# A diffusion-style block on one core: the second norm's factor at eviction, its shift as two extra columns of the up products

## The reference

```python
h  = rms(x, norm1_w) * (1 + scale1) + shift1
mixed = concat(s5(h @ w_in), attention(h @ w_in)) @ w_out
x  = x + gate1 * mixed
h2 = rms(x, norm2_w) * (1 + scale2) + shift2          # shift1 .. gate2 = silu(c) @ w_ada + b_ada
x  = x + gate2 * (silu(h2 @ w_ffn_gate) * (h2 @ w_ffn_up)) @ w_ffn_down     # "ffn1"
...                                                   # "ffn2", a pooling and attention mixer, "ffn3"

def _rms(x, w):
    y = x * lax.rsqrt(jnp.mean(x * x, axis=-1, keepdims=True) + 1e-6)
    return y * w
```

## Time and profile before

| | |
|---|---|
| median of 3 runs | 3241.77 us (3239.71 to 3243.99) |
| profiled execution | 3239.56 us |
| its span, mean granted clock of TensorE | 3237.8 us, 0.981 of full speed |
| read from memory | 627.53 MB, 194 GB/s over the span |

### The profile page before, as it was taken

How to read it: one execution, slowest core, us unless ns; L and a number is a source line. 1 busy time by engine, 2 the same in 40 slices (tenths; PEclk the granted TensorE clock), 3 DMA queues, 4 the chain that set the end, 5 groups by cost and what they waited for, 6 DMA issues and landing times.

```text
span 3237.8 us, 55997 instructions
## 1 busy us (share of the span) xinstructions
PE 3160.1 (98%) x24634; PEld 3021.9 (93%) x24634; DVE 1776.1 (55%) x1610; ACT 1236.9 (38%) x1162; POOL 153.3 (5%) x182
## 2 busy tenths in 40 slices
PE   6799999899999999999999999999999999999999
PEld 3599978899999999999999999999999998998997
DVE  0699865766444545654444544555556544454454
ACT  2376633433333333433333333343334333333333
POOL 1534100000000000000000000000030000000000
PEclk7799999999999999999999999999999999999999
DMA  9877667586555555555555555568635555555554
GB/s 343 295 252 239 240 228 239 194 279 226 184 184 191 183 184 192 174 178 171 180 170 179 170 177 174 174 181 148 129 128 183 181 189 180 190 181 189 188 181 156
DMA packets 329088, 631.88 MB, mean 195 GB/s; under 512 B 22452, under 2 KB 24264, under 8 KB 328664
## 3 DMA queue, kind: packets, MB, share of 16 engines
q1 hardware_dynamic: 317896, 626.16, 59.7%
q10 hardware_dynamic: 11040, 3.51, 0.5%
HBM read 627.53 MB, written 2.10 MB: 194 GB/s over the span
## 4 chain that ended last, share of the span: by engine, by line
PE 84%; DVE 2%; issue 1%; DMA 1%; ACT 1%; DVEq 0%; ACTq 0%
PE ps L576 21%; PE ps L577 21%; PE ps L578 21%; PE ps L606 3%; PE ps L608 3%; PE ps L607 3%; PE ps L2010 2%; PE ps L2012 2%; PE ps L2011 2%; PE ps L2047 1%; PE ps L2049 1%; PE ps L2048 1%; PE ps L1799 1%; PE ps L1800 1%; PE ps L1801 1%; DVE w_lo L443 1%
## 5 line engine op out<-in xcount | busy, mean ns | idle before, releaser
L443 DVE TENSOR_TENSOR w_lo<-raw,w_hi 128x2048 fp32r<-128x2048 f32 x496 | 1141.4, 2301 | 1246.5 <-ACT w_hi L438 1246.3
L438 ACT ACTIVATE w_hi<-raw 128x2048 fp32r<-128x2048 f32 x496 | 949.7, 1915 | 1700.9 <-PE ps L578 1308.7
L576 PE MATMUL ps<-act_hi,w_hi 128*128 128x256 f32 (+1 forms) x3328 | 949.8, 285 | 28.9 <-DVE act_lo L680 15.6
L577 PE MATMUL ps<-act_lo,w_hi 128*128 128x256 f32 (+1 forms) x3328 | 948.6, 285 | 0.0
L578 PE MATMUL ps<-act_hi,w_lo 128*128 128x256 f32 (+1 forms) x3328 | 946.8, 285 | 0.0
L576 PE MATMUL ps<-hid_hi,w_hi 128*128 128x256 f32 (+1 forms) x2816 | 795.8, 283 | 0.0
L577 PE MATMUL ps<-hid_lo,w_hi 128*128 128x256 f32 (+1 forms) x2816 | 795.4, 282 | 0.0
L578 PE MATMUL ps<-hid_hi,w_lo 128*128 128x256 f32 (+1 forms) x2816 | 794.3, 282 | 0.0
L576 PEld LDWEIGHTS ps<-act_hi,w_hi 128*128 128x128 f32 x3328 | 631.5, 190 | 31.1 <-issue 22.3
L577 PEld LDWEIGHTS ps<-act_lo,w_hi 128*128 128x128 f32 x3328 | 630.8, 190 | 0.0
L578 PEld LDWEIGHTS ps<-act_hi,w_lo 128*128 128x128 f32 x3328 | 630.6, 189 | 0.0
(11 more groups left out here) (370 smaller groups left out, 2754.2 us busy)
## 6 DMA issues: line engine op xcount, KB each, us to landing
...
```

Source lines behind the costliest of these rows:

```text
L438: act.activation(w_hi[b][:, :, :], raw[j % RING][:, :, :], ACT.Copy).then_inc(hi_ready, 1)
L443: dve.tensor_tensor(w_lo[b][:, :, :], raw[j % RING][:, :, :], w_hi[b][:, :, :].bitcast(F32), ALU.subtract).then_inc(lo_ready, 1)
L576: pe.matmul(o, whi, hi_, start=(k == 0 and not (shared and m % 2)), stop=False)
L577: pe.matmul(o, whi, lo_, start=False, stop=False)
```

## The change

The second norm is handled as the later ones: the products of `ffn1.up0`, `up1` and `up2` run on `res` times `gain` without `rstd`, and VectorE multiplies by `rstd` when either half is evicted. The shift has no place in that, so it is carried as a column of its own: the 16 columns ahead of the sequence are free in `act_hi` and `act_lo`, the last two of them (`SHIFT_COLS`) hold `shift2`, and all up products of `ffn1` have 258 moving columns (`UP1_COLS`). The result for the shift is column 1 of each bank. VectorE copies it to `up_bias` (`shift_out`); it is added as the bias of `Silu`, now four operations on `sig` in place of one from PSUM, and in the up half by four `scalar_tensor_tensor` in place of one product.

Quarters 0 and 1 of the norm's input are made behind the squares at `n` = 16 and 17 of `w_out` (`next_hi` on ScalarE, `next_lo` on VectorE), quarter 2 ahead of the split of the second chunk of `ffn1.up0` (`third_hi`), quarter 3 behind it. The four sums with `ones` stand ahead of the fourth chunk (`norm_pe`), mean and root at the fifth and sixth. Groups 2 and 3 of `w_out` are packed into banks 4 to 7 as 0 and 1 are in 0 to 3, and the last chunk is not run tile by tile any more. The gather of `scale2` moves from `n` = 18 to `n` = 14, into bank 0, and `gain` and the shift columns are made at `n` = 15 (`scale2_dve`). The diff, cut:

```diff
+SHIFT_COLS = slice(META - 2, META)
+UP1_COLS = slice(META - 2, T)
...
+        LATER = {"norm2": None, "ffn1_2": V_F1, "mix_2": V_MIX, "ffn2_2": V_F2}
+
+        def weight(name, k):
+            return gain[:, k:k + 1] if name == "norm2" else vecs[:, LATER[name] + k:LATER[name] + k + 1]
+
+        def normed_cols(name):
+            return SEQ_COLS if name == "norm2" else slice(0, T)
...
-                ins = act.activation(into(name)[0][:, k, :], res[:, k, :], ACT.Copy, scale=vecs[:, LATER[name] + k:LATER[name] + k + 1])
+                c = normed_cols(name)
+                ins = act.activation(into(name)[0][:, k, c], res[:, k, c], ACT.Copy, scale=weight(name, k))
...
-                q = hid0(p) + it
-                if deferred(p):
-                    act.wait_ge(bank_free[0], group_index(p, it, 0) + 1)
-                    n = cols.stop - cols.start
-                    act.activation(sig[:, :, 0:n], sig[:, :, 0:n], ACT.Silu).then_inc(sig_ready, 1)
-                    return
-                group_done(act, p, it, 0)
-
-                act.wait_ge(bank_free[1], group_index(p, it, 1))
-                act.activation(sig[:, :, 0:cols.stop - cols.start], bank(0, cols), ACT.Silu).then_inc(bank_free[0], 1)
-
-        def deferred(p):
-            return not p.name.startswith("ffn1")
+                n = cols.stop - cols.start
+                act.wait_ge(bank_free[0], group_index(p, it, 0) + 1)
+                if shifted(p):
+                    for m in range(4):
+                        ins = act.activation(sig[:, m, 0:n], sig[:, m, 0:n], ACT.Silu, bias=up_bias[:, 0, m:m + 1])
+                else:
+                    ins = act.activation(sig[:, :, 0:n], sig[:, :, 0:n], ACT.Silu)
+                ins.then_inc(sig_ready, 1)
+
+        def shifted(p):
+            return p.name.startswith("ffn1")
+
+        def up_bank(p, half, cols):
+
+            if shifted(p):
+                return ps[:, 4 * half:4 * half + 4, 2:2 + SEQ]
+            return bank(half, cols)
+
+        def shift_out(dve, p, half):
+            if shifted(p):
+                dve.tensor_copy(up_bias[:, half, :], ps[:, 4 * half:4 * half + 4, 1])
 
         def gate_dve(dve, p, it, g):
             cols = ffn_cols(p.name)
             n = cols.stop - cols.start
             q = hid0(p) + it
-            if g == 0 and deferred(p):
+            if g == 0:
 
                 group_done(dve, p, it, 0)
-                dve.wait_ge(hid_ready, q)
-                dve.tensor_tensor(sig[:, :, 0:n], bank(0, cols), per_token(cols), ALU.mult).then_inc(bank_free[0], 1)
+                if not (isinstance(q, int) and q == 0):
+                    dve.wait_ge(hid_ready, q)
+                shift_out(dve, p, 0)
+                dve.tensor_tensor(sig[:, :, 0:n], up_bank(p, 0, cols), per_token(cols), ALU.mult).then_inc(bank_free[0], 1)
             if g == 1:
                 group_done(dve, p, it, 1)
                 if not (isinstance(q, int) and q == 0):
                     dve.wait_ge(hid_ready, q)
-                if deferred(p):
-                    dve.tensor_tensor(val[:, :, 0:n], bank(1, cols), per_token(cols), ALU.mult).then_inc(bank_free[1], 1)
-                    dve.wait_ge(bank_free[1], group_index(p, it, 1) + 1)
-                    dve.wait_ge(sig_ready, q - sum(PARTS) + 1)
-                    dve.tensor_tensor(val[:, :, 0:n], sig[:, :, 0:n], val[:, :, 0:n], ALU.mult).then_inc(gate_mul, 1)
-                    dve.wait_ge(gate_mul, q - sum(PARTS) + 1)
+                shift_out(dve, p, 1)
+                dve.tensor_tensor(val[:, :, 0:n], up_bank(p, 1, cols), per_token(cols), ALU.mult).then_inc(bank_free[1], 1)
+                dve.wait_ge(bank_free[1], group_index(p, it, 1) + 1)
+                dve.wait_ge(sig_ready, q + 1)
+                if shifted(p):
+                    for m in range(4):
+                        ins = dve.scalar_tensor_tensor(out=val[:, m, 0:n], in0=val[:, m, 0:n], scalar=up_bias[:, 1, m:m + 1],
+                                                       in1=sig[:, m, 0:n], op0=ALU.add, op1=ALU.mult)
                 else:
-                    dve.wait_ge(bank_free[0], group_index(p, it, 0) + 1)
-                    dve.tensor_tensor(val[:, :, 0:n], sig[:, :, 0:n], bank(1, cols), ALU.mult).then_inc(bank_free[1], 1)
-                    dve.wait_ge(bank_free[1], group_index(p, it, 1) + 1)
+                    ins = dve.tensor_tensor(val[:, :, 0:n], sig[:, :, 0:n], val[:, :, 0:n], ALU.mult)
+                ins.then_inc(gate_mul, 1)
+                dve.wait_ge(gate_mul, q + 1)
...
                 cols = ffn_cols(f)
-                products(pe, f"{f}.up{i}", *((hid_hi, hid_lo) if f == "ffn3" else (act_hi, act_lo)), cols, counted(act_ready, ready0), norm if i == 0 else None)
+                if f == "ffn1" and i == 0:
+                    pe.wait_ge(gain_ready, 1)
+                    pe.wait_ge(shift_in, 2)
+                products(pe, f"{f}.up{i}", *((hid_hi, hid_lo) if f == "ffn3" else (act_hi, act_lo)), UP1_COLS if f == "ffn1" else cols,
+                         counted(act_ready, ready0), norm if i == 0 else None)
                 if f == "ffn3":
...
                 pending = run_phase(act, f"{f}.up{i}", split_hi, bind(act, gate_act), pending,
-                                    ahead={5: lambda: root_act(act, norm)} if norm and i == 0 else None)
+                                    ahead=({5: lambda: root_act(act, norm)} | ({1: lambda: third_hi(act)} if f == "ffn1" else {})) if i == 0 else None)
...
         def mean_root(dve, norm):
-            return {4: lambda: mean_dve(dve, norm, 4), 5: lambda: root_dve(dve, norm)}
+            return {4: lambda: mean_dve(dve, norm, 4), 5: lambda: root_dve(dve, norm)} | ({1: lambda: next_lo(dve, "norm2", 2)} if norm == "norm2" else {})
...
-            if g < 2:
-                return ps[:, 2 * g + m // 2, SEQ * (m % 2):SEQ * (m % 2) + SEQ]
-            return ps[:, (4, 0)[g - 2] + m, 0:SEQ]
+            return ps[:, 2 * g + m // 2, SEQ * (m % 2):SEQ * (m % 2) + SEQ]
 
         def first_free(g):
 
-            return bank_free[(0, 1, 1, 0)[g]], 1 + byname["w_out"].g0 // 2 + (1, 1, 2, 2)[g]
+            return bank_free[g // 2], 2 + byname["w_out"].g0 // 2 + g % 2
...
                 if n in (13, 14, 17):
-                    g = {13: 0, 14: 1, 17: 2}[n]
-                    act.wait_ge(*first_free(g))
-                    act.wait_ge(*((ssq_ready, QUADS + g) if g else (glu_mul, 2)))
-                    squares_act(act, g, 4 + g, T)
+                    first_squares(act, {13: 0, 14: 1, 17: 2}[n])
+                if n in (16, 17):
+                    act.wait_ge(gain_ready, 1)
+                    next_hi(act, "norm2", n - 16)
+
+        def first_squares(act, g):
+            act.wait_ge(*first_free(g))
+            act.wait_ge(*((ssq_ready, QUADS + g) if g else (glu_mul, 2)))
+            squares_act(act, g, 4 + g, T)
+
+        def third_hi(act):
+
+            act.wait_ge(chunk_done, byname["w_out"].before["S"] + 15)
+            next_hi(act, "norm2", 2)
 
...
+                    if n == 15:
+                        scale2_dve(dve)
+                    if n in (16, 17):
+                        next_lo(dve, "norm2", n - 16)
...
-            if m == 14:
-                pe.wait_ge(*first_free(2))
+            if m == 10:
+                pe.wait_ge(*first_free(0))
                 for g in range(4):
-                    gather(pe, accb2[:, g, :], 5, 4 * g)
-
-        def last_add(dve):
...
+        def scale2_dve(dve):
+
+            dve.wait_ge(mod_sum, 20)
+            link(dve, "dve", dve.tensor_tensor(gain[:, :], ps[:, 0, 0:16], bada[:, SCALE2:SCALE2 + 16], ALU.add))
+            link(dve, "dve", dve.tensor_scalar(gain[:, :], gain[:, :], 1.0, None, ALU.add))
+            dve.tensor_tensor(gain[:, :], gain[:, :], vecs[:, V_N2:V_N2 + 16], ALU.mult).then_inc(gain_ready, 1)
+            shift = mod[:, SHIFT2:SHIFT2 + KT].rearrange("p (k o) -> p k o", o=1).broadcast_to([P, KT, 2])
+            dve.tensor_copy(act_hi[:, :, SHIFT_COLS], shift).then_inc(shift_in, 1)
+            dve.wait_ge(shift_in, 1)
+            dve.tensor_tensor(act_lo[:, :, SHIFT_COLS], shift, act_hi[:, :, SHIFT_COLS].bitcast(F32), ALU.subtract).then_inc(shift_in, 1)
+            dve.wait_ge(gain_ready, 1)
...
-                pend = ffn_act(act, "ffn1", then(lambda: last_squares(act), lambda: norm_act(act, "norm2", 48)), squares_next_act(8, "ffn1_2"))
+                pend = ffn_act(act, "ffn1", then(lambda: first_squares(act, 3), lambda: next_hi(act, "norm2", 3)), squares_next_act(8, "ffn1_2"), "norm2")
...
-                pend = ffn_dve(dve, "ffn1", then(scale2, lambda: last_add(dve), lambda second: norm_dve(dve, "norm2", gain, 0, 48, second)), add_dve(("mod", 80)),
-                               squares_next_dve(8, "ffn1_2", add_dve(("mod", 80))))
```

(18 more changed lines are left out.)

56 lines of the change are left out of this document (13 added, 43 removed).

## The result

| | median us | range | runs |
|---|---|---|---|
| before | 3239.44 | 3237.18 to 3243.99 | 10 |
| changed | 3248.98 | 3242.93 to 3253.12 | 10 |

The ratio is 1.0030, 95% interval 1.0022 to 1.0039: slower by 9.5 us. 3248.0 was forecast, inside a range of 3237 to 3260. The profiled executions took 3239.56 and 3250.50 us, 10.9 apart, where the sum had given +6.2.

The account below looks back on a forecast made before the run. TensorE, busy 98% of the span, was taken to bound the kernel. 16.6 us removed against 19.6 added, plus 3.2 for the clock, made +6.2 on a median of 3241.77: 3248.0 us, range 3237 to 3260.

Parts of the forecast that it names:

- norm off the path, half clock, second pause: From the end of `w_out` into `ffn1.up0`: pauses and half-clock stretches around the second norm go, 16.6 us removed.
- two columns: All 4224 up products of `ffn1`: 258 columns instead of 256, on a straight line to 272, add 4.1 us.
- wait at `n` = 18: Last chunk but one of `w_out`: four `next_hi` ahead of its `w_hi` make TensorE wait 1.7 us.
- three boundaries with an ada chunk: Iteration boundaries of `ffn1.up0`: longer up-half eviction with an ada chunk grows the pause from 1.5 to 3.3, 5.5 us in all.
- seven S2 waits: Third chunk at seven later boundaries of `up1`, `up2` and their down parts: longer up-half eviction adds 4.0 us.
- eleven S6 waits: Seventh chunk of an iteration, behind the gate's eviction: four Silus instead of one delay it, eleven times, 4.0 us.
- first pass: Start of `ffn1.up0`: an addition, a sum of squares and an ada step ahead of the third chunk's `w_lo`, 0.3 us.
- clock behind three pauses: Behind the three longer pauses of `ffn1.up0`: half clock after two of three, 3.2 us, bounds 0 and 4.8.
- gather at its new place: In `w_out` at `n` = 14: costs the same 3.5 us and half-clock stretch as at its old place.
- column as the unit: Up products of `ffn1`: a product steps by single columns, 0.49 ns each, so two cost 0.98 ns per product.
- columns charged in steps: Rival for `ffn1`'s up products: 258 columns handled as 272, 29 us on top, time 3277; chance 0.13.
- all three: Rival: all three longer pauses of `ffn1.up0` lose the clock, 4.8 us instead of 3.2, time 3249.6; chance 0.12.

Follow-up runs that it names:

- Experiment 1: Changed kernel with other numbers and starts of moving columns (256 to 272) in the three up parts of `ffn1`; three single runs: 3251.2, 3257.6 and 3247.04 us.
- experiments 2: Changed kernel with one `Silu` without the gate's shift in `up1` and one product without the up half's shift in `up2`; 3244.64 us, single run.
- 3: Ada chunks of `up0` moved so that none stands behind an eviction: on the changed kernel 3237.31 us, on the kernel before 3234.75 us.
- 5: Changed kernel with VectorE's up-phase evictions in two pieces, the product by `rstd` ahead of the second chunk's split; 3233.04 us, 0.9975 of before.
- 4: Changed kernel with quarter 1 of the norm's input made one chunk later, at `n` = 18 behind that chunk's split; 3245.1 us, single run.
- experiment 7: Changed kernel with later ada chunks, two-piece evictions, quarter 1 at `n` = 18, and gather products spread behind each three products; 3222.58 us, 0.9944 of before.

## Why the prediction was right, and where its terms were off

The time is right to 1 us, and part of that is luck. The forecast added 6.2 us to a median of three runs, 3241.77; over ten runs that median is 3239.44, 2.3 lower. The difference came out as 9.5 us in the medians and 10.9 in the profiled executions, so the sum itself was 3 to 5 us short. Within the sum, errors of either sign partly cancel too. By terms, from the profiled executions:

| term | forecast | measured |
|---|---|---|
| norm off the path, half clock, second pause | -16.6 | -16.5 |
| two columns | +4.1 | +7.7 |
| wait at `n` = 18 | +1.7 | +1.8 |
| three boundaries with an ada chunk | +5.5 | +4.8 |
| seven S2 waits | +4.0 | +3.8 |
| eleven S6 waits | +4.0 | +2.4 |
| first pass | +0.3 | +0.2 |
| clock behind three pauses | +3.2 | +4.3 |
| gather at its new place | 0 | +1.6 |
| sum | +6.2 | +10.1 |

The traces differ by 10.9; 0.6 of it stands ahead of all that the change touches, at the start of `n` = 12, and 0.2 is in no row.

*Removed.* From the end of `w_out` to the end of S3 the kernel before took 40.9 us (569.60 to 610.52) and the changed one 25.0 (573.61 to 598.62); with 0.35 for the columns of four chunks and 0.2 for the first pass, which lie inside it, that is 16.5. Nothing came late in its place.

*Two columns* was the term mis-sized most, by its straight line: 0.09 us a chunk, not 0.047. Experiment 1 says why. The "column as the unit" was right for 260 and 264 to 0.02 us, and 258 from 14 pays 0.04 over the line for its place. The bound that was kept, the full price of 272 (33 us), stayed far off: the rival of columns charged in steps is out. The Trainium skill, "TensorE: Matmul & The Clock Gate", section "Wait — 56ns, not 53.3ns?", gives time by the number of columns alone; four different times for 256 columns here do not agree with it.

*The gate's eviction at S5* was sized too high, 0.36 for 0.22. The Silus cost what was said (1.62 against the 1.6 forecast), the slack was larger than the 0.48 read in `ffn3.up`, since a chunk of 258 lasts 0.09 longer; the rest of the difference, some 0.05, was not traced.

*The boundaries* were within 0.7 and 0.2 us. With the ada chunk VectorE's chain grew from 3.35 us to 5.13 (678.08 to 683.21 in the changed kernel), by 1.78 where 1.89 was forecast, and the old pause had cost 1.6, not 1.5. For the seven others 0.6 seven times less 0.3 twice is 3.6, not the 4.0 written; 3.8 was measured. The order of the queues and the rows of `ffn3.up` carried them, and experiments 2, 3 and 5 each took away the waits that the text had put down to their part.

*The clock* was "two of three, 3.2". In this trace it was two of three, but one stretch at 0.50 was longer than the other (2.7 and 1.6 us lost). Over six profiled executions that have the three pauses, 2.9 to 3.1 us each (the changed kernel, experiments 1, 2 and 4), fifteen of eighteen came with 1.2 GHz; the mean loss is 4.2 us an execution. The rival "all three", 4.8, was nearer than the forecast, but that every long pause pays did not hold: three of 2.96 to 3.12 us kept 2.4 GHz. What decides it was not tried.

*The gather* was costed as the same at its new place. The chunk with it took 10.72 us at `n` = 18 before, and 12.33 at `n` = 14 here, since the half clock began inside the sixteen products. In the nine profiles that have it at `n` = 14 in a row it was 12.3 six times and 10.7 three times, so this is scatter and no fixed price; in those three the forecast's "same" held. In experiment 7, with the products spread, the half clock does not appear.

*The chances.* The bound of 6.5 us lay just above the forecast of +6.2, and the measured +9.5 lies above it: by the forecast's own bound the outcome is "slower", which had 0.43, not "same", which had 0.51.

The change itself was not at fault so much as what it put on VectorE: with evictions in two pieces, ada chunks later and quarter 1 at `n` = 18 it gives 3225.4, where the kernel before with the same ada order has 3234.75. Of these 9.4 us 1.9 are `ffn3`'s, which the two pieces could give the kernel before as well; that was not run.
